# Five norms of a three-block transformer kernel: chunks 0 and 1 first, part of a weight split moved to GpSimd, two halves of another moved in VectorE's order

## What is computed

```
h  = x + rms_norm(merged @ w_out, g_post_mix)
gu = rms_norm(h, g_pre_ffn) @ w_gate_up                 # norm 1: gate_up0
h  = h + rms_norm(ff, g_post_ffn)
proj = h @ attn_w_in                                    # norm 2: attn_in
x = layer_norm(ALPHA * x + attention @ attn_w_out, ...)
y = square(relu(x @ ffn_w_up)) @ ffn_w_down             # norm 3: up_a0
x = layer_norm(ALPHA * x + y, ...)
q, f, i = split(x @ hgrn_w_in)                          # norm 4: hgrn_in
x = layer_norm(ALPHA * x + hgrn @ hgrn_w_out, ...)
y = square(relu(x @ ffn_w_up)) @ ffn_w_down             # norm 5: up_h0
x = layer_norm(ALPHA * x + y, ...)                      # the last norm: output
```

## Time and profile before

| what | value |
|---|---|
| median of 3 runs | 2201.03 us |
| the profiled execution's own time | 2198.23 us |
| its span on the core | 2196.4 us |
| TensorE matmul busy | 2112.0 us (96%) |
| VectorE busy | 1235.3 us (56%) |
| ScalarE busy | 905.6 us (41%) |
| GpSimd busy | 69.4 us (3%) |
| chain that ended last | PE 86%, DVE 7%, DVEq 3%, ACT 2%, issue 2% |

### The profile page before, as it was taken

How to read it: one execution, slowest core, us unless ns; L and a number is a source line. 1 busy time by engine, 2 the same in 40 slices (tenths; PEclk the granted TensorE clock), 3 DMA queues, 4 the chain that set the end, 5 groups by cost and what they waited for, 6 DMA issues and landing times.

```text
span 2196.4 us, 29669 instructions
## 1 busy us (share of the span) xinstructions
PE 2112.0 (96%) x11082; PEld 1724.9 (79%) x11082; DVE 1235.3 (56%) x2051; ACT 905.6 (41%) x1400; POOL 69.4 (3%) x63
## 2 busy tenths in 40 slices
PE   6999999999999999999989999999999999999997
PEld 5777788888877888888877788888778877888886
DVE  7986444334455666666666642344567676423444
ACT  7244332222246656556553531232355534312322
POOL 1000200000220000000000000000000000000000
PEclk9998999999999999999999999999999999999998
DMA  4012222232232221212221222222111222232221
GB/s 172 21 40 98 75 96 86 86 115 88 84 105 87 78 87 49 86 67 79 75 77 44 96 96 96 96 95 96 58 58 59 94 77 77 97 105 89 99 93 53
DMA packets 31232, 182.96 MB, mean 83 GB/s; under 512 B 5152, under 2 KB 5536, under 8 KB 12448
## 3 DMA queue, kind: packets, MB, share of 16 engines
q1 hardware_dynamic: 28656, 177.95, 23.1%
q10 hardware_dynamic: 1584, 3.71, 0.5%
q0 software_dynamic: 896, 0.06, 0.0%
HBM read 179.54 MB, written 2.10 MB: 83 GB/s over the span
## 4 chain that ended last, share of the span: by engine, by line
PE 86%; DVE 7%; DVEq 3%; ACT 2%; issue 2%; DMA 0%; ACTq 0%
PE ps L593 12%; PE ps L591 12%; PE ps L592 12%; PE ps L1113 5%; PE ps L1115 5%; PE ps L1114 5%; PE ps L1169 3%; PE ps L1171 3%; PE ps L1170 3%; PE ps L1215 2%; PE ps L1217 2%; PE ps L1216 2%; PE ps L652 1%; PE ps L642 1%; PE ps L621 1%
## 5 line engine op out<-in xcount | busy, mean ns | idle before, releaser
L1350 ACT ACTIVATE w_hi<-raw 128x2048 fp32r<-128x2048 f32 (+1 forms) x122 | 225.9, 1852 | 294.6 <-PE ps L593 220.2
L591 PE MATMUL ps<-x_hi,w_lo 128*128 128x512 f32 x816 | 317.6, 389 | 0.5 <-DVE y L2289 0.3
L593 PE MATMUL ps<-x_hi,w_hi 128*128 128x512 f32 x816 | 317.5, 389 | 0.0
L592 PE MATMUL ps<-x_lo,w_hi 128*128 128x512 f32 x816 | 317.4, 389 | 0.0
L1815 DVE TENSOR_TENSOR w_lo<-raw,w_hi 128x2048 fp32r<-128x2048 f32 (+3 forms) x116 | 259.3, 2235 | 93.5 <-ACT w_hi L1350 92.9
L1113 PE MATMUL ps<-x_hi,w_lo 128*128 128x512 f32 x544 | 218.9, 402 | 2.9 <-DVE w_lo L2459 2.4
L1115 PE MATMUL ps<-x_hi,w_hi 128*128 128x512 f32 x544 | 213.1, 392 | 0.0
L1114 PE MATMUL ps<-x_lo,w_hi 128*128 128x512 f32 x544 | 212.4, 390 | 0.0
L591 PEld LDWEIGHTS ps<-x_hi,w_lo 128*128 128x128 f32 x816 | 153.2, 188 | 32.9 <-issue 0.7
L592 PEld LDWEIGHTS ps<-x_lo,w_hi 128*128 128x128 f32 x816 | 153.2, 188 | 32.0
L593 PEld LDWEIGHTS ps<-x_hi,w_hi 128*128 128x128 f32 x816 | 153.1, 188 | 31.8
(11 more groups left out here) (467 smaller groups left out, 3907.2 us busy)
## 6 DMA issues: line engine op xcount, KB each, us to landing
raw<-w_attn_in SPq DMA_DIRECT2D x32, 1024.0 KB, 4.9
raw<-w_gate_up SPq DMA_DIRECT2D x22, 1024.0 KB, 4.8
raw<-w_up_a SPq DMA_DIRECT2D x16, 1024.0 KB, 4.9
raw<-w_down_a SPq DMA_DIRECT2D x16, 1024.0 KB, 4.9
raw<-w_up_h SPq DMA_DIRECT2D x16, 1024.0 KB, 4.9
raw<-w_down_h SPq DMA_DIRECT2D x16, 1024.0 KB, 4.9
raw<-w_hgrn_in SPq DMA_DIRECT2D x8, 1024.0 KB, 4.9
raw<-w_down SPq DMA_DIRECT2D x8, 768.0 KB, 4.2
```

Source lines behind the costliest of these rows:

```text
L591: pe.matmul(o, w_lo[:, slot, a:a + P], hi[:, k, :], start=k == 0, stop=False)
L592: pe.matmul(o, w_hi[:, slot, a:a + P], lo[:, k, :], start=False, stop=False)
L593: last = pe.matmul(o, w_hi[:, slot, a:a + P], hi[:, k, :], start=False, stop=k == st.kc - 1)
L1350: act.activation(w_hi[:, slot, 0:width], raw[:, slot, 0:width], ACT.Copy).then_inc(whi_ready, 1)
```

## The change

- `second_lo` of 2 x 1024 columns on VectorE is replaced by `begin_lo` on VectorE, which makes only the blocks of chunks 0 and 1 (2 x 256 columns; 256 for hgrn_in), and by `second_lo` on GpSimd, which makes chunks 2 to 7 (2 x 768 columns; 768 for hgrn_in) in one instruction as soon as the high part is there. TensorE waits for the new `lo_begun` at pair (1,0) and for `wlo_ready` at pair (1,2). GpSimd raises `wlo_ready` once both parts are made.
- `layer_norm` with a projection behind it has a new order on VectorE: the scale multiplies of chunks 0 and 1 side by side, then `h` and `x_lo` of both, then `begin_lo`, and the mean is subtracted one chunk ahead instead of two.
- ScalarE makes `x_hi` ahead of `h`, and signals `h` with the new `h_made`.
- In the two norms behind an out projection `next_lo(0)` runs ahead of the wait for the last tile, and `next_lo(1)` takes its old place behind the last residual add.
- The last norm keeps its order (`last_chunks`).

```diff
+            def second_lo(name):
+                n0 = STAGES[name].slab0 + 1
+                pool.wait_ge(whi_ready, n0 + 1)
+                low, whole, high = (of_chunks(buf[:, n0 % 2, :], name, 2, DC) for buf in (w_lo, raw, w_hi))
+                pool.tensor_tensor(low, whole, high.bitcast(f32), ALU.subtract)
+                pool.drain()
+                pool.wait_ge(wlo_ready, n0)
+                pool.wait_ge(lo_begun, LO_BEGUN[name])
+                pool.sem_inc(wlo_ready, 1)
...
-                    if k == 0:
+                    if (c, k) == (1, 0):
+                        pe.wait_ge(lo_begun, LO_BEGUN[st.name])
+                    elif (c, k) in ((0, 0), (1, 2)):
                         pe.wait_ge(wlo_ready, st.slab0 + c + 1)
...
-                    if c > 1 or not after:
-                        last = act.activation(h[:, c, :], y[:, c, :], ACT.Identity, scale=g, bias=b)
                     if after:
                         act.activation(x_hi[:, c, :], y[:, c, :], ACT.Identity, scale=g, bias=b).then_inc(xhi_ready, 1)
+                    if c > 1 or not after:
+                        act.activation(h[:, c, :], y[:, c, :], ACT.Identity, scale=g, bias=b) \
+                           .then_inc(h_made if after else result_ready, 1)
...
+                        if paired and t == DC - 1:
+                            next_lo(st, 0)
                         dve.wait_ge(tile_done, st.tile0 + t + 1)
...
                 if paired:
-                    next_lo(st, 0)
+                    next_lo(st, 1)
...
-                if part == "mix":
-                    next_lo(STAGES[{"a": "attn_out", "h": "hgrn_out"}[layer]], 1)
...
+                for c in range(2):
+                    tt(y[:, c, :], y[:, c, :], scale, ALU.mult).then_inc(y_ready, 1)
+                settle()
+                for c in range(2):
+                    ts(h[:, c, :], y[:, c, :], gain(...), gain(...), ALU.mult, ALU.add)
+                    settle()
+                    part_lo(after, c, h[:, c, :])
+                begin_lo("hgrn_in" if after == "hgrn_in" else after + "0")
+                tt(y[:, 2, :], y[:, 2, :], mean, ALU.subtract)
+                settle()
+                for c in range(2, DC):
+                    tt(y[:, c, :], y[:, c, :], scale, ALU.mult).then_inc(y_ready, 1)
+                    if c + 1 < DC:
+                        tt(y[:, c + 1, :], y[:, c + 1, :], mean, ALU.subtract)
+                    if c > 2:
+                        chunk_lo(after, c - 1)
+                    settle()
+                chunk_lo(after, DC - 1)
+            def chunk_lo(after, c):
+                dve.wait_ge(h_made, H_MADE[after] + c - 1)
+                part_lo(after, c, h[:, c, :])
```

More of the change, by code:

```diff
@@ L318, in build @@
     xhi_ready = sem("xhi_ready")
+    h_made = sem("h_made")
+    lo_begun = sem("lo_begun")
     xlo_ready = sem("xlo_ready")
@@ L436, in fold_at, with of_chunks @@
         return (DC - 1, st.kc - 6 if st.body[0] == 1 else st.kc - 2)
+    LO_BEGUN = {"gate_up0": 1, "attn_in": 2, "up_a0": 3, "hgrn_in": 4, "up_h0": 5}
+    def of_chunks(slab, name, k0, k1):
+        tiles = 1 if name == "hgrn_in" else 2
+        return slab[:, 0:tiles * DC * P].rearrange("p (m a) -> p m a", m=tiles)[:, :, k0 * P:k1 * P]
+    H_MADE = {"up_a": 0, "hgrn_in": DC - 2, "up_h": 2 * (DC - 2)}
     def joins(p):
@@ L563, in send @@
                     pool.dma_start(far_stat[:, b, :, :], class_stat[32 * b:32 * b + 32, old, :, :, :]).then_inc(far_ready, 16)
-            for name, event in ACCS[:2]:
-                accumulate(name, event)
+            def second_lo(name):
[7 more added lines that the diff above has]
+                pool.sem_inc(wlo_ready, 1)
+            accumulate(*ACCS[0])
+            second_lo("gate_up0")
+            accumulate(*ACCS[1])
+            second_lo("attn_in")
             send(0, 0)
@@ L570, in _ @@
                 send(2 * i + 2, 0)
+            for name in ("up_a0", "hgrn_in", "up_h0"):
+                second_lo(name)
         @block.tensor
@@ L1816, in split_lo, with begin_lo @@
                     .then_inc(wlo_ready, 1)
-            def second_lo(name, half):
+            def begin_lo(name):
                 n0 = STAGES[name].slab0 + 1
-                slot = n0 % 2
-                cols = slice(SLAB // 2 * half, SLAB // 2 * half + SLAB // 2)
                 dve.wait_ge(whi_ready, n0 + 1)
-                last = tt(w_lo[:, slot, cols], raw[:, slot, cols], w_hi[:, slot, cols].bitcast(f32), ALU.subtract)
-                if half == 1 or name == "hgrn_in":
-                    last.then_inc(wlo_ready, 1)
+                low, whole, high = (of_chunks(buf[:, n0 % 2, :], name, 0, 2) for buf in (w_lo, raw, w_hi))
+                tt(low, whole, high.bitcast(f32), ALU.subtract).then_inc(lo_begun, 1)
             def next_lo(st, half):
@@ L2591, in layer_norm, with last_chunks @@
                 dve.wait_ge(rstd_spread, NTH_SPREAD[var] + 1)
+                if not after:
+                    last_chunks(mean, scale)
+                    return
+                for c in range(2):
+                    tt(y[:, c, :], y[:, c, :], scale, ALU.mult).then_inc(y_ready, 1)
+                settle()
+                for c in range(2):
+                    ts(h[:, c, :], y[:, c, :], gain(f"ln_{part}_g{n}", c), gain(f"ln_{part}_b{n}", c), ALU.mult, ALU.add)
+                    settle()
[14 more added lines that the diff above has]
+                part_lo(after, c, h[:, c, :])
+            def last_chunks(mean, scale):
                 for c in range(DC):
@@ L2595, in layer_norm @@
                         tt(y[:, c + 2, :], y[:, c + 2, :], mean, ALU.subtract)
-                    if after and c < 2:
                         settle()
[L2598 to L2609, removed]
             def norm_and_ffn(layer, proj, up, down, n, after):
```

14 lines of the change are left out of this document (7 added, 7 removed).

## The result

| kernel | median, us | lowest and highest | runs |
|---|---|---|---|
| before | 2200.78 | 2197.78 to 2202.32 | 20 |
| changed | 2203.97 | 2202.43 to 2205.93 | 20 |

A forecast was written before the change was run, and what follows sets the result against it. TensorE, busy 96% of the span, was taken to bound the kernel, so only its waits count. Terms + 3.1 + 2.7 - 1.8 - 2.1 = + 1.9 us gave 2203 us from the median of before, 8 in 10 range 2198.5 to 2208 us.

The forecast's parts named there:

- Turns: In the norms, GpSimd and VectorE each wait for the other's whole instruction; VectorE operations reading one operand from PSUM pass.
- the rival in which turns don't bind: GpSimd gives way or leaves gaps, so norms 1 and 2 lose nothing: -6.3 us, 2194.7 us; chance 8%.
- GpSimd's instruction: The new low-part instruction in each norm takes 3.6 us for 1536 columns and 1.9 us for 768.
- The rival of a slow GpSimd: In the four norms with 1536 columns GpSimd takes longer than 3.6 us; at 4.6 us, 2207.4 us; chance 22%.
- Norm 2: attn_in: GpSimd starts ahead of the first residual add, which ends 3.1 us later, and TensorE's first matmul with it.
- Norm 1: gate_up0: GpSimd ties with the first residual add; a loss of 2.7 us, between branches, bounds 0.6 and 3.3.
- the branch in which it wins: In norm 1 GpSimd wins the tie, and the residual add ends 3.3 us later.
- Norm 3: up_a0: the `next_lo` move and an earlier `x_lo` of chunk 4 outweigh GpSimd's hold of `h`; a gain of 0.9 us.
- VectorE's pitch sets the tail: In norms 3 and 5 VectorE's 1.98 us a chunk against TensorE's 1.36 us a pair; gain follows chunk 4's `x_lo`, 0.8 us.
- 2.1 us for a norm without GpSimd's hold: Norms 3 and 5 would each gain 0.67 + 0.8 + 0.65 = 2.1 us without GpSimd's turn.
- Norm 4: hgrn_in: nobody waits for GpSimd and the 1.99 us wait for `x_hi` of chunk 2 goes; gain 2.1 us, bounds 1.5 and 2.3.
- Norm 5: up_h0: like norm 3 to 0.1 us, so also a gain of 0.9 us.

The follow-up runs named there:

- e1: The changed kernel with GpSimd's instruction cut from 1536 (768) columns to 8, leaving out most of the second slab's low part: 2193.06 us.
- e5: The changed kernel with GpSimd's instruction in pieces of 512 columns (256 in norm 4), begun at the same point: 2200.87 us.
- e6: The kernel before with only the move of `next_lo` ahead of the last chunk's residual in the layer norms: 2199.56 us.
- e7: The kernel before, unchanged, run for a third profile, which fell in the upper group of its run times: 2201.25 us.
- e9: The kernel of e4 run once more, unchanged: 2192.32 us.
- e4: The changed kernel with norms 1 and 2 as before, and GpSimd in norms 3 to 5 also waiting for `lo_begun`: 2192.33 us.
- e2: The changed kernel with norms 1 and 2 as before (VectorE makes all of `w_lo`), norms 3 to 5 as changed: 2197.96 us.
- e0: The kernel before, unchanged, run for a second profile: 2200.49 us.
- e8: As e2, but without GpSimd's share: in norms 3 to 5 VectorE makes the columns of chunks 2 to 7 itself: 2197.6 us.

## Why the forecast came out, step by step

- **Turns: right.** Each engine stands for the whole instruction of the other; the rival in which turns don't bind (2194.7 us) is out, as the adds of 3.82 and 3.59 us and e1 show. Right too that in norms 3 and 5 both multiplies pass and only `h` stands.
- **GpSimd's instruction: right**, 3.42 us for 3.6 and 1.81 for 1.9. The rival of a slow GpSimd (from 4.15 us on) is out.
- **Norm 2: the mechanism right, the size in part by luck**, 3.1 us measured and forecast. The add takes 2.9 us longer (3.59 less 0.69) and not 3.1, as GpSimd's instruction was shorter than forecast; the other 0.2 us comes behind it, in pairs that run longer at 1.2 GHz, which was in no term.
- **Norm 1: the term was mis-sized**, 3.2 us for the 2.7 that I took between the branches. GpSimd began at 251.89, 0.15 us ahead of the add at 252.04, and won; the branch in which it wins had 3.3. The tie is real: in e5, where it began at 252.42 and the add at 252.40, VectorE won and the norm lost 2.1.
- **Norm 3: the number right, the path not.** It is -0.8 for -0.9, and e6 shows its first part alone (0.62 of 0.67). For the rest I had said that VectorE's pitch sets the tail, so that the norm gains what `x_lo` of chunk 4 gains. Here are that `x_lo` and the matmuls that read it, VectorE and TensorE after:

```profile
1235.49 0.69 DVE L1864 TENSOR_TENSOR x_lo<-h,x_hi 128x512 fp32r<-128x512 f32 x1
...
1236.60 0.62 PE L680 MATMUL ps<-x_lo,w_hi 128*128 128x512 f32 x2
```

It starts 19.35 us behind the last add (at 1216.14), against 20.43 before: 1.1 us earlier. But TensorE comes to it only 0.4 us after it is done (1236.18), and waits for no `x_lo` behind chunk 0's. TensorE's own pace sets the end of the norm, and it ran at 1.2 GHz until 1230 (0.50 granted from 1228 to 1230). So -0.8 is what was left of the gain at that clock. In e7 the granted clock over norm 3 is 0.85 as well, and the norm takes the time of before (0.0): there TensorE waits for VectorE anyway, which hides the slow stretch.

The prediction's 2.1 us for a norm without GpSimd's hold was too small: e1 gains 3.3 and 3.2 us in norms 3 and 5, e9 2.8 and 3.0. I had counted the waits as the list has them. TensorE's timeline before, the starts of three pairs in a row:

```profile
1225.53 0.63 PE L642 MATMUL ps<-x_hi,w_hi 128*128 128x512 f32 x2
...
1227.52 0.62 PE L642 MATMUL ps<-x_hi,w_hi 128*128 128x512 f32 x2
...
1229.49 0.62 PE L642 MATMUL ps<-x_hi,w_hi 128*128 128x512 f32 x2
```

A pair with a listed wait of 0.3 us takes 1.99 and 1.97 us, against 1.36 undisturbed: it costs 0.6 us, twice what is listed.

- **Norm 4: mis-sized**, -1.7 for -2.1. The wait for `x_hi` of chunk 2 went, but TensorE stands 0.51 us for `x_lo`, and VectorE stands 0.47 us ahead of its multiply at 1588.65, which I had not in the sum. That norm came out 0.8 and 1.5 us apart in kernels that have it as before (e7, e6), so its size is not sure to better than that.
- **Norm 5: the step failed that said it is like norm 3 to 0.1 us**: +0.5 for -0.9. The waits are alike (0.8 and 1.0 us for `x_lo`, `h` held 2.41 and 2.77 us); the clock is not. Busy time by stretch, before and then after; the figure behind POOL's is the granted clock:

```profile
1819.00:1821.00 2.00, 1.02 (x7) 0.78 (x7) 1.98 (x5) 1.78 (x2) 0.00 (x0) 0.80 0.02 4
...
1825.00:1827.00 2.00, 2.00 (x6) 1.36 (x5) 1.85 (x4) 0.82 (x1) 0.00 (x0) 0.50 0.00 0
1827.00:1829.00 2.00, 1.59 (x7) 0.95 (x5) 2.00 (x3) 0.00 (x0) 0.00 (x0) 0.99 0.00 0
```

```profile
1824.00:1826.00 2.00, 2.00 (x12) 2.00 (x12) 0.49 (x3) 0.07 (x1) 0.00 (x0) 0.56 0.57 119
...
1836.00:1838.00 2.00, 2.00 (x7) 1.53 (x6) 1.93 (x4) 2.00 (x4) 0.00 (x0) 0.53 0.82 328
1838.00:1840.00 2.00, 2.00 (x11) 1.64 (x10) 1.91 (x4) 1.59 (x4) 0.00 (x0) 1.00 0.36 147
```

Before, TensorE is at 1.2 GHz from 1820 to 1827, and 3.6 us of that are matmuls of the pairs. After, it is so from 1824, while it still makes the statistics, to 1838. So the reciprocal comes 4.6 us behind the last add, against 4.7 before and 4.0 in norm 3: what the move of `next_lo` gives is gone before the pairs start. And 7.3 us of the pairs' matmuls run at the lower clock, which no wait for VectorE hides any more. From the last add to the end of the norm the granted clock is 0.90 before, 0.80 after and 0.85 in norm 3 of after. What the order gained, the clock took. Two profiles of one kernel differ as much there: e4 and e9 gain 1.7 and 3.0 us (granted 0.84 and 0.89).

- **What the sum left out** is, above all, the clock. The norms measure 3.2 + 3.1 - 0.8 - 1.7 + 0.5 = 4.3 us, 2.4 above the forecast (0.5 in norm 1, 0.1 in norm 3, 0.4 in norm 4 and 1.4 in norm 5), and 1.4 and 0.9 us lie outside them. I had put the base at the median of before and the sum on it, which cancelled the part of this that before's upper group has as well: against e7, of that group, attention is the same and norm 5 is 0.1 us longer. So 1.9 against 3.2 us is closer than the steps were, and that is luck.
- **Open**: what decides, with like waits, whether TensorE gets the lower clock, and so how much of the clock's part is the change's (its 20 runs have the lowest granted clock of all kernels here, with e2's and e5's slower runs) and how much is chance. And whether pieces help by themselves in norms 1 and 2, since the tie fell to VectorE in the same run.

## What to carry to other kernels

Before giving part of VectorE's work to GpSimd, list what VectorE does in the next 3.5 us: an SBUF-only operation there stands still for the whole of GpSimd's instruction, one with a PSUM operand does not. Start GpSimd's share by a signal from VectorE when the PSUM stretch begins, not as soon as its inputs are there; here this one wait turned a loss of 3.2 us into a gain of 4.6. Price a wait of TensorE by the distance between like matmuls, not by the listed idle time. And take a gain from several profiles of either kernel where TensorE's waits are a few us: the same wait may cost a stretch at half clock in one execution and none in the next.

## What the runs showed that I had not expected

- Which of the two wins the tie in norms 1 and 2 follows TensorE's clock one step earlier: the first add comes 1.92 and 2.22 us behind the reciprocal in the changed kernel, and 1.75 and 1.83 us in e5, while GpSimd starts at 1.77 and 1.84 us in both.
- Three GpSimd instructions of 512 columns take 5.17 us in norms 1 and 2, in alternation with VectorE, and 3.92 in norm 3, where VectorE reads PSUM beside the first and stands for most of the other two; one of 1536 takes 3.42. One of 8 columns takes 0.20 us, and 0.66 where it waits for VectorE's add.
- Like waits of 2.2 and 0.8 to 0.9 us at one place left TensorE at 2.4 GHz in five of the twelve profiles (the first of before, e0, e4, e6, e8) and at 1.2 GHz in the other seven, of before and of changed kernels.
